# Context's V rows of tile 1 and the second keys/values moved into a reordered last mixer, the layer-1 modulation divided, both expert choices ahead of the first attention

## What is computed

```python
mod = (silu(c) @ w_mod[l] + b_mod[l])            # shift, scale, gate: twice
xn = modulate(rms_norm(h, norm1_g[l]), mod[:, 0], mod[:, 1])
p = xn @ w_in[l]                                 # q k v, pool, conv, gates
o = diff_attention(q, [k, kc], [v, vc])          # keys/values of x and of context
merged = g0 * attn_norm(o) + g1 * pool + g2 * conv
h = h + mod[:, 2] * (merged @ w_out[l])
# peer: per token and head the top 16 of 256 candidates
hid = gelu(einsum('td,thkd->thk', x, u_emb[eidx]))      # the U rows
y = einsum('thk,thkd->td', gate * hid, v_emb[eidx])     # the V rows
h = h + mod[:, 5] * y
```

## Time and profile before

| what | us |
|---|---|
| median of 3 runs | 3791.75 |
| their range | 3781.43 to 3808.75 |
| the profiled execution: its time | 3771.84 |
| its span, from first to last instruction | 3770.1 |

### The profile page before, as it was taken

One profiled execution on the slowest core, in us unless ns is written; L12 is line 12 of the kernel. 1 busy time (PEld: TensorE's weight loads), 2 busy tenths in 40 slices (PEclk: granted clock), 3 DMA queues, 4 the chain that ended last, 5 costly groups with the idle time before them and its releaser, 6 DMA issues.

```text
span 3770.1 us, 31121 instructions
## 1 busy us (share of the span) xinstructions
PE 2773.1 (74%) x10826; PEld 1552.4 (41%) x10826; DVE 2218.0 (59%) x4294; ACT 588.5 (16%) x1409; POOL 1693.6 (45%) x1556
## 2 busy tenths in 40 slices
PE   6999997348797788796248772989899920687388
PEld 3557585224543334646123220434466720332133
DVE  1321169987577898737979448224511398954732
ACT  1220010011421220011002110221400100111021
POOL 0000025466464568503575777750000057677776
PEclk8999998579898899998578996999999965899799
DMA  6654479999898889957798999974144579899999
GB/s 209 234 205 147 150 265 392 399 320 359 310 340 312 302 282 399 380 190 278 229 405 313 384 409 401 376 301 145 45 145 139 178 260 341 322 368 409 409 377 366
DMA packets 402342, 1111.92 MB, mean 295 GB/s; under 512 B 37139, under 2 KB 91603, under 8 KB 401420
## 3 DMA queue, kind: packets, MB, share of 16 engines
q0 software_dynamic: 223024, 811.71, 57.4%
q1 hardware_dynamic: 179164, 298.22, 22.5%
HBM read 1105.52 MB, written 4.29 MB: 294 GB/s over the span
## 4 chain that ended last, share of the span: by engine, by line
PE 48%; DVE 15%; POOL 15%; DMA 11%; issue 8%; ACT 2%; SPq 0%; DVEq 0%; ACTq 0%; POOLq 0%
PE PS L472 30%; POOL ring L1052 15%; PE PS L540 13%; DVE ring L1419 5%; DMA ring<-in_peer_u,eidx 3%; DMA ring<-in_peer_v,eidx 2%; DMA wring<-in_w_mod 2%; DMA wring<-in_w_in 2%; DVE acc L1425 1%; DVE work L1498 1%; PE PS L561 1%; ACT work L1067 1%; DVE work L1504 1%; PE PS L741 1%; DVE work L1914 1%
## 5 line engine op out<-in xcount | busy, mean ns | idle before, releaser
L1052 POOL DMA_INDIRECT ring<-in_peer_u,eidx x768 | 852.8, 1110 | 1520.8 <-DVE work L1910 490.3
L540 PE MATMUL PS<-ring,diag 128*128 128x512 f32 x1984 | 916.2, 608 | 525.9 <-ACT diag L1092 413.9
L1419 DVE SCALAR_TENSOR_TENSOR ring<-ring,xn_peer 128x1024 f32<-128x1024 f32 x768 | 933.0, 1221 | 326.2 <-DMA ring<-in_peer_u,eidx 318.0
L1052 POOL DMA_INDIRECT ring<-in_peer_v,eidx x768 | 830.8, 1082 | 394.9 <-issue 178.3
L540 PEld LDWEIGHTS PS<-ring,diag 128*128 128x128 f32 x1984 | 364.7, 192 | 1054.3 <-ACT diag L1092 623.1
L472 PE MATMUL PS<-wring,xnT 128*128 128x512 f32 (+2 forms) x1728 | 737.1, 588 | 21.7 <-issue 12.7
L1425 DVE SCALAR_TENSOR_TENSOR acc<-ring,small,acc 128x1024 f32<-128x1024 f32 x268 | 343.9, 1283 | 297.7 <-DMA ring<-in_peer_v,eidx 286.9
L472 PE MATMUL PS<-xnT,wring 128*128 128x128 f32 (+1 forms) x2896 | 489.2, 331 | 40.3 <-DMA wring<-in_w_in 26.8
L472 PEld LDWEIGHTS PS<-wring,xnT 128*128 128x128 f32 x1728 | 330.4, 194 | 420.6 <-issue 412.3
L472 PEld LDWEIGHTS PS<-xnT,wring 128*128 128x128 f32 x2896 | 443.4, 196 | 85.3 <-DMA wring<-in_w_in 30.1
L1067 ACT ACTIVATE work<-PS 128x512 f32<-128x512 f32 (+5 forms) x377 | 187.9, 529 | 1073.6 <-PE PS L472 760.2
(11 more groups left out here) (169 smaller groups left out, 1562.5 us busy)
## 6 DMA issues: line engine op xcount, KB each, us to landing
wring<-in_w_in SPq DMA_DIRECT2D x128, 1024.0 KB, 7.4
wring<-in_w_mod SPq DMA_DIRECT2D x48, 1024.0 KB, 14.0
wring<-in_peer_wq SPq DMA_DIRECT2D x24, 1024.0 KB, 5.1
wring<-in_ab_w_in SPq DMA_DIRECT2D x13, 1024.0 KB, 23.1
wring<-in_conv_out_w SPq DMA_DIRECT2D x12, 1024.0 KB, 5.1
wring<-in_w_out SPq DMA_DIRECT2D x12, 1024.0 KB, 7.4
ring<-in_peer_u,eidx POOLq DMA_INDIRECT x768, 6.6
ring<-in_peer_v,eidx POOLq DMA_INDIRECT x768, 6.6
```

What stands on the lines that cost most here:

```text
L540: ins = pe.matmul(PS[:, b + c, :], diag[:, state["summed"] % ND, :], ring[:, m % NG, 512 * c:512 * c + 512], start=(k == SUMS[r, t][0]), s ...
L1052: pool.indirect_dma_start(ring[:, m % NG, :], None, tables[kind], bass.IndirectOffsetOnAxis(ap=eidx[:, r % 2, t, k:k + 1], axis=0))\
L1419: v.scalar_tensor_tensor(out=slot, in0=slot, scalar=1.0, in1=xn_peer[:, t, :], op0=ALU.mult, op1=ALU.mult, accum_out=hid[:, t, k:k + 1]).t ...
```

## The change

Nothing is computed otherwise; work is moved and split.

- The 128 V rows of the context's tile 1 and their gate are taken out of mixer 1 and put after run 1's items, on DVE, beside the last mixer (stage "m2": 0.3 rows per operation, 6 per product). Their weights are held in a tile `held` until then.
- mixer(3) goes into the last mixer. Its order is now q, k, v; u, pool, g1, convolution, co, g2 (`branches`); then norm, k, v of 3; then the attention, g0, out.
- The modulation of layer 1 is divided: its first 4 products go one by one into mixer 0's convolution, the other 8 into the last mixer's attention, one at every other unit.
- The U rows of tile 0 lie thinner beside the choices (0.15), 5 per unit in the ab attention, then at 0.3; the rest are forced at "heads c", ahead of the c attention, where gelu of tile 0 follows.
- V rows of tile 0: 0 to 39 in the c units, 40 to 87 in mixer 1's units, 88 to 127 after it; 96 instead of 80 of them on DVE. U rows of tile 1: 80 up to mixer 1's attention, 48 after it. gelu of tile 1 comes after g1 of mixer 1.
- In run 1, tile 0 is weighed right after its choice, and tile 1 is chosen after that, as run 2 does already.

```diff
-PACE = {"front0": 0.35, "ab": 0.8, "c": 0.8, "m1": 0.7, "m3": 0.8, "front1": 0.35, "front2": 0.35}
+PACE = {"front0": 0.15, "ab": 0.3, "c": 0.8, "m1": 0.7, "front1": 0.35, "m2": 0.3, "front2": 0.35}
-PER_PRODUCT = {"ab": 6, "c": 6, "m1": 5, "m3": 16}
+PER_PRODUCT = {"c": 6, "m1": 5, "m2": 6}
-SUMS_PER_UNIT = {"ab": 2, "c": 2, 1: 1}
+SUMS_PER_UNIT = {"c": 2, 1: 1}
-TURN_AT = {"ab": (0, 0), "heads 1": (0, 1)}
+TURN_AT = {"heads c": (0, 0), "g1 1": (0, 1)}
+SOFTMAX_AT = {"gated c": (0, 1)}
...
+            if r == 0:
+                halves("mod1_0", "w_mod", 1, 2 * WB * n, 2 * WB * (n + 1), 2 * n)
...
+        if r == 2:
+            branches(r, l)
+            qkv(3, l, "kv")
+            halves("mod1_1", "w_mod", 1, 2 * D, 6 * D)
...
-        a, b = 8 * ROWS_PER_UNIT["ab"], 8 * (ROWS_PER_UNIT["ab"] + ROWS_PER_UNIT["c"])
-        U1_EARLY = 50
+        a, b = 8 * ROWS_PER_UNIT["c"], 8 * ROWS_PER_UNIT["c"] + 16 * ROWS_PER_UNIT[1]
+        U1_EARLY = 80
...
-        items(0, "v", 1)
-        items(0, "gate", 1, 0, 1)
...
+            if r == 1:
+                items(0, "v", 1)
+                items(0, "gate", 1, 0, 1)
...
-                modulation(1, 0)
-                modulation(1, 1)
...
+                    if r == 0:
+                        modulation(1, 0, n)
...
+                if r == 2:
+                    branches(r)
+                    turn_norm(("m", 3))
+                    wait_norm(("m", 3))
+                    qkv(3, "kv")
...
-                attention(r, M_UNITS, scores, turns, values, modulate if r == 0 else None)
+                attention(r, M_UNITS, scores, turns, values, modulate if r != 1 else None)
...
-                rows_upto(0, "u", 1, U1_EARLY - 1)
+                turn_to_v("heads c")
                 pace(None)
...
+                if r == 2:
+                    branches(r)
+                    rows_upto(0, "gate", 1, 0)
+                    norm(("m", 3), H["c"], "n1_3", [], "sc_3", "sh_3")
+                    head_norms(3, "kv")
...
             choose_tile(1, 0)
-            top_scale(1, 0)
-            pace("m3")
-            mixer(3, [("product", "xnT", ("m", 1), T - 1, 1)])
+            weigh(1, 0)
             pace(None)
-            gelu_first(1, 0)
-            gelu_last(1, 0)
             choose_tile(1, 1)
             weigh(1, 1)
             rows_upto(1, "gate", 1, 0)
-            mixer(2, [("product", "xnT", ("m", 3), T - 1, 1)])
+            rows_free(0, "gate", 1, 0)
+            pace("m2")
+            mixer(2, [("product", "xnT", ("m", 1), T - 1, 1)])
```

More of the change, by code:

```diff
@@ L149, in qkv, with branches @@
                 halves(f"{name}{r}", "w_in", l, off, off + D)
-    def mixer(r, l, first="qkv"):
-        qkv(r, l, first)
-        halves(f"g0{r}", "w_in", l, 7 * D, 8 * D)
+    def branches(r, l):
         halves(f"u{r}", "w_in", l, 3 * D, 4 * D)
@@ L1273, in heads_in, with branches @@
                                 put_turned(("kT", r, t), 8, KT[:, 0 if RUN[r][1] == "x" else 1, :, :], t)
+            def branches(r):
+                for m in range(2):
+                    for t in range(T):
+                        act.wait_ge(*at("product", "u", r, t, m))
+                        copy(TOK[:, t, 512 * m:512 * m + 512], bank("u", r, t, m), "read", "u", r, t, m)
+                for c in range(KD // 2):
+                    act.wait_ge(*at("product", "poolT", r, c))
+                    copy(POOLTS[r][:, 2 * c:2 * c + 2, :], bank("poolT", r, c).rearrange("p (a b) -> p a b", a=2), "read", "poolT", r, c)
+                turn(f"pooled {r}")
+                gates(("g1", r))
+                turn(f"g1 {r}")
+                for n in range(4):
+                    act.wait_ge(*at("product", "ch", r, n))
+                    if n == 0:
+                        act.wait_ge(*at("gate_read", gate_sigmoid.count - 1))
+                    if n:
+                        act.wait_ge(*at("conv_in", r, n - 1))
+                    copy(E[:, 0:512], bank("ch", r, n), "read", "ch", r, n)
+                    if r == 0:
+                        modulation(1, 0, n)
+                for n in range(2):
+                    for t in range(T):
+                        if n == 0 and t == 0:
+                            act.wait_ge(*at("convT", r, KD - 1))
+                        gate_sigmoid(("g2", r), t, n)
             def mixer(r, before):
@@ L1279, in mixer @@
                 norm_turn(("m", r))
-                if r in (0, 3):
+                if r in (0, 2):
                     act.wait_ge(*at("lam_dots", r))
                     A(act.activation(lam2[:, :], lam2[:, :], ACT.Exp), "lam_exp", r)
-                heads_in(r, "kv" if r == 3 else "qkv", l)
-                if r == 3:
-                    return
+                heads_in(r, "qkv", l)
                 turn(f"heads {r}")
+                if r == 2:
+                    branches(r)
+                    norm(("m", 3), H["c"], [("h_peer", 0, T - 1), ("gate_read", gate_sigmoid.count - 1)])
+                    norm_turn(("m", 3))
+                    heads_in(3, "kv", l)
                 for u in range(len(M_UNITS) + 2):
@@ L1313, in mixer @@
                 gates(("g0", r))
[L1314 to L1335 removed]
+                if r != 2:
+                    branches(r)
                 if r == 0:
@@ L1852, in mixer, with branches @@
                         e = gate(("g0", r), t, n, False)
-                        mul(MERGED[:, t, 512 * n:512 * n + 512], O_TOK[:, t, 512 * n:512 * n + 512], e)
-                        gate_done(("g0", r), t, n)
-                beside(4)
+                        o, m = o_tok[:, t, 512 * n:512 * n + 512], merged[:, t, 512 * n:512 * n + 512]
+                        if r == 2:
+                            mul(o, o, e)
+                            add(m, m, o)
+                        else:
+                            mul(m, o, e)
+                        gate_done(("g0", r), t, n)
+                        if r == 2 and n == 1:
+                            same("dve", "merged", r, t)
+                if r != 2:
+                    beside(4)
+                    branches(r)
+            def branches(r):
+                merged, convt = MERGEDS[r], CONVTS[r]
+                scaled = merged if r == 2 else O_TOK
                 v.wait_ge(*row_wait(f"ps_{r}"))
@@ L2015, in _ @@
                 choose_tile(0, t, norm_ab)
-            for t in range(T):
-                top_scale(0, t)
+            top_scale(0, 0)
             first_block()
```

291 lines of the change are left out of this document (139 added, 152 removed).

## The result

The changed kernel takes 3816.4 us (median of 16 runs, 3803.8 to 3843.2) beside 3792.4 for the kernel before in the same runs (16 runs, 3777.2 to 3808.8): ratio 1.0075, 95% interval 1.0052 to 1.0097. That is within 1%, and a loss of 20 to 37 us. The forecast was 3808. The profiled execution has a span of 3814.2 us; against before's 3770.1 that is +44, of which 20 are the distance of before's profile to its own median.

A forecast was written before the change was run, and what follows sets the result against it. No single limit: DVE bounds the choice, DMA the rows of runs 1 and 2 and mixer 1's convolution, PE the last mixer. Terms: -108 up to the last mixer, +124 in it, +16: 3791.75 to 3808 us, range 3765 to 3850.

The forecast's parts named there:

- 8d: Last mixer's branches: DVE is late when the convolution starts and row gathers press on its weights, +12 us (0 to 45).
- 8a: Last mixer's attention: eight modulation products at 2.3 us each stand among PE's work, +18 us (5 to 25).
- 8c: Last mixer's q, k, v with rows: DVE is late with k's norm and PE waits, +18 us (8 to 25).
- 2: The context's choice with fewer U rows beside it: -65 us, and -28 us behind it, before the ab attention.
- 6: Mixer 1 after its attention: PE's waits go once the rows run out at the 89th, -18 us (0 to 34).
- 8b: Last mixer: norm, k, v and turns of mixer(3) now stand on the path, +76 us.
- 7: Run 1's front and rows: the new order takes run 2's time, -33 us (28 to 36).
- 1: Mixer 0's convolution: four modulation products at 2.3 us each, +9 us, up to 15 if a load came late.
- 3: The ab attention: five U rows per unit on DVE make it 75 us, -3 us, or up to +10.
- first rival: Last mixer: unbroken rows starve its weights, the convolution takes 120.1 us; sum +51, 3843 us; chance 2 in 10.
- contention costs nothing: Whole kernel: DMA contention costs nothing anywhere; sum -22, 3770 us, or another -12, 3758; chance 1.5 in 10.
- modulation late: Last attention: the divided modulation's 16 MB of loads fall behind and PE waits; +10, 3818 us; chance 1 in 10.

The follow-up runs named there:

- e4: The kernel before with only the new order of run 1 and of the last mixer: 3834.8 us, ratio 1.0109 to the kernel before.
- e1: The changed kernel with 0.8 instead of 0.3 U rows per operation between the ab and c attention: ratio 1.0037 to the kernel before.
- e2: The changed kernel with layer 1's twelve modulation products back in the first block, ahead of the ab attention: ratio 1.0012 to the kernel before.
- e3: The changed kernel without 127 of the 128 V rows of tile 1 in the last mixer (output lacks them): ratio 0.9973 to the kernel before.
- e6: The changed kernel with the same 128 V rows spread evenly over the last mixer, second chip: ratio 1.0081 to the kernel before.
- e8: The changed kernel with e2, e5 and e6 together and the last mixer's rows ten earlier, third chip: ratio 0.9913 to the kernel before.
- e5: The changed kernel with six U rows beside each of four ab gate and output products, second chip: ratio 0.9999 to the kernel before.

## Why the prediction was right, and where its steps failed

The forecast of no change beyond 1% held, and so did the range and the likeliest case's own (+24 between the medians against +16). Part of this is luck: in the last mixer 8d came out 15 us above its forecast and 8a and 8c together 14 below, so that the total, 127.6 against 124, is better than its terms. By its steps:

- **Right, with their size:** the choice and what lies behind it (2), the chain to the c attention (4), mixer 1 (6: the 89th row was the right mark, its convolution took 100.3), and mixer(3) on the path (8b). e4 confirms 8b by itself: 76.6 against 76.
- **7, run 1, right in direction, its size not shown.** One pair of profiles gives -32.2. From first choice to last row before has 813.2 us and the changed kernel 779.8, but the same order has 797.0 in e1, 798.9 in e2, 786.0 in e3 and 794.6 in e4: -14 to -33, -22 in the mean. The kernel before has only the one profile, itself 20 us below its median. The prediction called this its best founded term, 28 to 36.
- **1, mixer 0, too small.** The four products take the 9.3 us of the sum; 6 more are a wait of co for its weights (3.1 us) and what follows more slowly; that the blocks now put between others cause it is not shown by itself, but e2, which takes them out again, starts the choice 14.5 us earlier. The prediction had this as its upper bound, 15, and chose the lower end.
- **3, the ab attention, wrong in sign but small.** DVE's five rows per unit did not fit the 75 us; it took 78.6.
- **8a, the divided modulation, too large:** +10.5, not +18. The price of one product was right where it is paid. DVE's score reductions in the middle of the attention, of the changed kernel and then of e2 without the products, begin 9.3 us and 7.1 us apart over two units, so a product costs 2.2:

```profile
2881.04 1.23 DVE L1848 TENSOR_REDUCE small<-PS 128x2 f32<-128x1024 f32 x1 [0.42 <-PE PS L798]
...
2890.38 1.22 DVE L1848 TENSOR_REDUCE small<-PS 128x2 f32<-128x1024 f32 x1 [0.42 <-PE PS L798]
```

```profile
2883.97 1.23 DVE L1847 TENSOR_REDUCE small<-PS 128x2 f32<-128x1024 f32 x1 [0.42 <-PE PS L796]
...
2891.07 1.23 DVE L1847 TENSOR_REDUCE small<-PS 128x2 f32<-128x1024 f32 x1 [0.42 <-PE PS L796]
```

But only five of the eight are paid so. The first two fall into waits at the attention's start (from the first reduction to the fifth 14.3 us in the changed kernel, 14.2 in e2), and the last, behind the last reduction, costs 1.2. The term had a bound of 5 for products in gaps and no row to choose by.
- **8c, the mechanism was wrong.** It had DVE late with the norm of k. In PE's timeline the products themselves are longer, 94.4 us from the first of q to the last of v instead of e3's 84.04, and the turns of k wait for DVE for only 1.55:

```profile
2446.82 30.03 PE L493 MATMUL PS<-wring,xnT 128*128 128x512 f32 x64 [0.94 <-ACT xnT L1095]
2479.15 41.44 PE L493 MATMUL PS<-wring,xnT 128*128 128x512 f32 x96 [2.29 <-issue]
2524.47 16.72 PE L493 MATMUL PS<-wring,xnT 128*128 128x512 f32 x32 [3.88 <-issue]
...
2545.37 1.09 PE L501 MATMUL PS<-const,work 128*128 128x128 f32 x8 [1.55 <-DVE work L1533]
```

The gaps are put down to issue, but e3 takes away only rows and the gaps go with them: they are waits for weights. The weight blocks issued in this stretch take 10.9 us from issue to landing in the median, in e3 6.4:

```profile
wring<-in_w_in SPq DMA_DIRECT2D x10, 1024.0 KB, 10.9
```

```profile
wring<-in_w_in SPq DMA_DIRECT2D x10, 1024.0 KB, 6.4
```

Of the two blocks issued from 2506.9 us one takes 17.1 us to land, at 2524.4, where the third row of PE's timeline above begins.
- **8d, the size was wrong: +26.7, not +12.** The convolution was to hold 34 rows and held 42, since eight were still owed by the gates ahead, and its loss is 18.4 us. The prediction set the point of decision at one row per 2 us; 42 in 101 us is one per 2.4, and it costs. e6 with 19 rows and e8 with 23, each on another chip, still wait and take 90.4 us, 7 more than without rows. So the first rival's mechanism is real and was paid by half; what it got wrong is its one rate as the point of decision: the loss is 0 without rows, 7 with 19 to 23, 18 with 42.
- **What the prediction did not see:** two prices of the change can be had back. That PE would idle 99 us ahead of the ab attention follows from steps 2 and 8a, yet the modulation was costed where the change put it; and the forced U rows were costed without asking which waits of DVE beside them stood empty.

The other two rivals: "contention costs nothing" is ruled out by e3; "modulation late" asked for more than 18 us in the attention, and taking the products out in e2 gives back 11.3.

The equal packet counts of the earlier trace rows held only roughly in the last mixer's convolution. The DMA queues of the changed kernel from 2622 to 2675 us (packets, MB, share):

```profile
q0 software_dynamic: 4164, 15.13, 73.5%
q1 hardware_dynamic: 5524, 5.57, 30.5%
```

The weights get 105 GB/s where PE wants 145, although they have a third more packets than the gathers. The Trainium skill's rule of turns packet by packet ("DMA: Bandwidth & Descriptors", section "Queues, rings and completion order") thus gives the direction at most: a load of 1 KB lines beside one of 4 KB rows gets far less than half. By that section a packet is typically some 9 to 17 descriptors, and no run here shows whether the packets that the profile counts, of about 1 KB and 3.6 KB, are these; so the equal counts of the earlier trace rows did not confirm the rule as firmly as the prediction has it. The measured counts decide the size.

## What to carry to other kernels

Rows or loads that fill an idle stage are not free there: ask what share of DMA the stage's own weights need, above all where their lines are short, and expect a gradual loss (here 38 us for 128 rows in 340 us). Fillers on an in-order engine belong inside its waits for other engines, counted place by place; behind the operations of a dependent chain they give back half, and left for the end they give back all (e6). When a change shortens one engine's stretch, look which other engine now idles there, and cost the work that was moved away against that hole before accepting where it went; but check what is queued behind it there (e8's exponential), since a hole that just fits on one chip may not on another.

## What the runs showed of the hardware

- Chips differ in gather bandwidth. In e8, on the third chip, run 1's rows take 570.4 us, on the first 531.9 in the changed kernel, with nearly the same instructions; the second chip is like the third (569.9 in e5). The kernel before is 1.6 to 1.9% slower on these two.

```profile
1865.80:2436.20 570.40, 418.65 (x896) 165.81 (x896) 279.73 (x558) 88.91 (x226) 406.51 (x387) 0.91 0.96 355
```

- Even on one chip stages with identical code spread between executions: run 2's front took 245.4 to 257.8 us over six profiles (before, after, e1 to e4) and run 1 in its new order 779.8 to 798.9 over five. The +11.6 of run 2 in the table lies within this spread: a term below 10 us can't be read from one pair of profiles there.
- Products put into an idle stretch run slow and are still free as long as they end before what the stretch waits for. In e2's first block PE, busy 45 of 87 us with waits of some 4 us between the products, was granted 0.56 of full speed, near the lower level of 1.2 GHz, and a product took 3.64 us instead of the 1.96 that the first one took behind a gapless stretch.
